# Attention heads' outputs made transposed, with the probabilities scaled before they are turned

## What is computed

```python
# block 0: 8 MoBA heads (with 256 rows: causal softmax attention) and 8 stick-breaking heads
y_a = softmax(mask(q_a @ k_a.T * 64**-0.5)) @ v_a                  # per head, HEAD_DIM 64
A[t,s] = sigmoid(z[t,s]) * prod_{s<j<t} (1 - sigmoid(z[t,j])); y_b = A @ v_b
merged = sigmoid(g_a) * (y_a @ w_branch_moba) + sigmoid(g_b) * (y_b @ w_branch_sb)
x = x + merged @ w_out
# block 1: 8 "fox" heads (softmax with cumulative log-forget bias), 8 "dsa" heads
# (softmax over the 64 best keys of an index score, one shared k and v), same merge
```

## Time and profile before

| | us |
|---|---|
| median of 3 runs (1128.9 to 1129.7) | 1128.99 |
| the profiled execution | 1129.26 |
| its span, first to last instruction | 1127.5 |
| PE busy | 1119.7 |
| DVE busy | 770.7 |
| ACT busy | 621.2 |
| POOL busy | 60.2 |

### The profile page before, as it was taken

One profiled execution on the slowest core, in us unless ns is written; L12 is line 12 of the kernel. 1 busy time (PEld: TensorE's weight loads), 2 busy tenths in 40 slices (PEclk: granted clock), 3 DMA queues, 4 the chain that ended last, 5 costly groups with the idle time before them and its releaser, 6 DMA issues.

```text
span 1127.5 us, 15022 instructions
## 1 busy us (share of the span) xinstructions
PE 1119.7 (99%) x5926; PEld 959.9 (85%) x5926; DVE 770.7 (68%) x1070; ACT 621.2 (55%) x843; POOL 60.2 (5%) x105
## 2 busy tenths in 40 slices
PE   9999999999999999999999999999999999999998
PEld 8888888888888888888888888888788888888887
DVE  6777755754887777775487777457897487777742
ACT  5555532677556456554365555337676864655530
POOL 1000000000000000000000000020253100000000
PEclk9999999999999999999999999999999999999999
DMA  9755565653454565655665555556643445565551
GB/s 316 245 188 188 187 243 192 204 177 119 159 196 149 176 217 187 187 187 187 189 203 186 187 187 188 188 173 248 206 148 115 149 152 184 188 187 187 189 184 38
DMA packets 142581, 208.03 MB, mean 185 GB/s; under 512 B 9296, under 2 KB 100584, under 8 KB 142512
## 3 DMA queue, kind: packets, MB, share of 16 engines
q1 hardware_dynamic: 139408, 198.07, 53.8%
q0 software_dynamic: 3088, 9.00, 2.4%
q10 hardware_dynamic: 16, 0.00, 0.0%
HBM read 205.98 MB, written 2.65 MB: 185 GB/s over the span
## 4 chain that ended last, share of the span: by engine, by line
PE 95%; DVE 2%; ACT 1%; issue 1%; DMA 1%; SPq 0%; ACTq 0%; DVEq 0%
PE banks L1770 26%; PE banks L1631 16%; PE banks L1633 16%; PE banks L1632 16%; PE banks L1768 13%; PE banks L1703 1%; PE banks L1653 1%; PE banks L1918 1%; PE banks L1945 1%; PE banks L1946 1%; DVE w_lo L1107 1%; DMA raw<-in_ffn_w_gate 1%; PE banks L1905 0%; PE banks L1944 0%; PE banks L1872 0%
## 5 line engine op out<-in xcount | busy, mean ns | idle before, releaser
L1107 DVE TENSOR_TENSOR w_lo<-raw,w_hi 128x2048 fp32r<-128x2048 f32 x186 | 423.4, 2279 | 171.9 <-ACT w_hi L731 171.4
L731 ACT ACTIVATE w_hi<-raw 128x2048 fp32r<-128x2048 f32 x186 | 352.7, 1898 | 115.6 <-PE banks L1633 112.1
L1770 PE MATMUL banks<-xT,w_hi 128*128 128x512 f32 x1280 | 313.6, 391 | 0.0
L1770 PEld LDWEIGHTS banks<-xT,w_hi 128*128 128x128 f32 x1280 | 232.6, 189 | 43.3
L1631 PE MATMUL banks<-w_hi,xT 128*128 128x512 f32 (+1 forms) x464 | 183.2, 395 | 1.2 <-DVE w_lo L1107 1.2
L1633 PE MATMUL banks<-w_hi,xT 128*128 128x512 f32 (+1 forms) x464 | 179.3, 387 | 0.0
L1632 PE MATMUL banks<-w_lo,xT 128*128 128x512 f32 (+1 forms) x464 | 179.1, 386 | 0.0
L1768 PEld LDWEIGHTS banks<-xT,w_lo 128*128 128x128 f32 x1280 | 169.9, 191 | 9.6
L1768 PE MATMUL banks<-xT,w_lo 128*128 128x256 f32 x1280 | 173.6, 283 | 0.0
L1631 PE MATMUL banks<-w_hi,hT_hi 128*128 128x512 f32 x352 | 137.3, 390 | 0.0
L1633 PE MATMUL banks<-w_hi,hT_lo 128*128 128x512 f32 x352 | 137.0, 389 | 0.0
(11 more groups left out here) (302 smaller groups left out, 926.1 us busy)
## 6 DMA issues: line engine op xcount, KB each, us to landing
raw<-in_ffn_w_gate SPq DMA_DIRECT2D x88, 512.0 KB, 4.0
raw<-in_ffn_w_up SPq DMA_DIRECT2D x88, 512.0 KB, 5.0
raw<-in_ffn_w_down SPq DMA_DIRECT2D x88, 512.0 KB, 4.3
raw<-in_w_in SPq DMA_DIRECT2D x76, 512.0 KB, 4.6
raw<-in_w_out SPq DMA_DIRECT2D x16, 512.0 KB, 4.4
raw<-in_w_branch_moba SPq DMA_DIRECT2D x4, 512.0 KB, 4.7
raw<-in_w_branch_sb SPq DMA_DIRECT2D x4, 512.0 KB, 6.0
raw<-in_w_branch_a SPq DMA_DIRECT2D x4, 512.0 KB, 4.4
```

Source lines behind the costliest of these rows:

```text
L731: act.activation(w_hi[u % SLOTS][:, 0:n], raw[u % RAWS][:, 0:n], ACT.Copy).then_inc(hi_done, 1)
L1107: dve.tensor_tensor(w_lo[r][:, 0:n], raw[r][:, 0:n], w_hi[u % SLOTS][:, 0:n], ALU.subtract).then_inc(lo_done, 1)
L1770: m = pe.matmul(bank[b + s], mh, xT[:, k].rearrange("p a s -> p (a s)"), start=k == 0, stop=k == KC - 1)
```

## The change

The values become the stationary operand of a head's product: two heads' values side by side, 128 columns (for dsa, whose value is shared, the value twice), so that the output of a head appears transposed, on the 64 partitions of its half, as 256 columns. The first product takes 256 columns of the turned probabilities, the second 128. The reciprocal can't be applied to rows of a transposed output any more, so the probabilities are multiplied by it before they are transposed: on DVE right behind the reciprocal for moba and dsa, on ACT for fox. Transposing, product and copy-out stand one slot later. The copy-out is one copy of 64 x 256 without a factor, for both kinds of heads. PE's transpositions of the branches and their bank reads go; ACT and DVE round and split the collected outputs from SBUF, in two halves a branch, in the slots `Y_AT`.

```diff
-TY_AT = (38, 43)
+Y_AT = [(37, 38, 40, 42), (37, 38, 40, 43)]
@@ items_of
-    out += [(TY_AT[0], "TY", (0, 0)), (TY_AT[0] + 1, "TY", (0, 1)), (TY_AT[1], "TY", (1, 0)), (TY_AT[1], "TY", (1, 1))]
@@
-SM_AT = dict(soft=1, turn=2, out=3, norm=4)
+SM_AT = dict(soft=1, exp=2, scale=3, turn=3, out=4, norm=5)
@@ ACT
-                            mv(dv[:, tt, :], src[:, 72:136])
+                            mv(dv[:, tt, 0:HD], src[:, 72:136])
+                            mv(dv[:, tt, HD:2 * HD], src[:, 72:136])
+                def scale_probs(it):
+                    k, e = 2 * (it.m % 8), prob[it.m % 2]
+                    act.wait_ge(inverted, it.softs + 1)
+                    act.activation(e[:, 0:P], e[:, 0:P], ACT.Copy, scale=rowinv[:, k:k + 1])
+                    act.activation(e[:, P:SC], e[:, P:SC], ACT.Copy, scale=rowinv[:, k + 1:k + 2]).then_inc(scaled_a, 1)
                 def finish_head(it):
...
                     act.wait_ge(head_out, it.m + 1)
-                    if it.kind == "SM":
-                        k = 2 * (it.m % 8)
-                        act.wait_ge(inverted, it.softs + 1)
-                        act.activation(y[br][:, 0, c], O[:, 0:HD], ACT.Copy, scale=rowinv[:, k:k + 1])
-                        act.activation(y[br][:, 1, c], O[:, HD:P], ACT.Copy, scale=rowinv[:, k + 1:k + 2])\
-                            .then_inc(head_read, 1)
...
+                    act.activation(y_cols[br][r, h // 2, :], head_bank(it)[r, 0:SEQ], ACT.Copy).then_inc(head_read, 1)
-                def y_turned(it):
...
+                def y_round(br, n):
+                    heads = [it for it in HEADS if it.b == b and branch_of(it) == br]
+                    act.wait_ge(head_read, heads[4 * n + 3].m + 1)
                     if br == 1:
                         act.wait_ge(unit_used, BASE[ph] + 2 * PROJ)
...
+                    k = slice(2 * n, 2 * n + 2)
+                    act.activation(yT_hi[br][:, k, :], y_cols[br][:, k, :], ACT.Copy).then_inc(y_hi, 1)
@@ ACT, loop over slots: copy_turned, finish_head, then
+                    if slot in Y_AT[b]:
+                        y_round(*divmod(Y_AT[b].index(slot), 2))
...
                     for it in ITEMS[b]:
-                        if it.kind == "SM" and slot - it.slot == SM_AT["turn"]:
+                        if it.kind == "SM" and slot - it.slot == SM_AT["exp"]:
                             exps(it)
+                    for it in ITEMS[b]:
+                        if it.kind == "SM" and it.what[0] == "fox" and slot - it.slot == SM_AT["scale"]:
+                            scale_probs(it)
@@ DVE
                     dve.reciprocal(rowinv[:, k:k + 2], rowsum[:, k:k + 2]).then_inc(inverted, 1)
+                    if it.what[0] != "fox":
+                        e = prob[it.m % 2]
+                        dve.wait_ge(inverted, it.softs + 1)
+                        dve.tensor_scalar(e[:, 0:P], e[:, 0:P], rowinv[:, k:k + 1], None, ALU.mult)
+                        dve.tensor_scalar(e[:, P:SC], e[:, P:SC], rowinv[:, k + 1:k + 2], None, ALU.mult)\
+                            .then_inc(scaled_d, 1)
+                def y_rest(br, n):
+                    dve.wait_ge(y_hi, 4 * b + 2 * br + n + 1)
...
-                        if it.kind == "TY" and d == 1:
-                            y_turned(it)
+                    if slot in Y_AT[b][0:3]:
+                        y_rest(*divmod(Y_AT[b].index(slot), 2))
...
                         merge(0, (0, 1))
+                        y_rest(1, 1)
@@ PE
                 def turn_probs(it):
-                    pe.wait_ge(exped, it.softs + 1)
+                    if it.what[0] == "fox":
+                        pe.wait_ge(scaled_a, it.what[1] + 1)
+                    else:
+                        pe.wait_ge(scaled_d, 8 * b + it.what[1] + 1)
@@ PE, head
-                    O = head_bank(it)[:, SC:NB]
-                    pe.matmul(O[:, 0:HD], w[:, 0:P], v[:, 0, :], start=True, stop=True)
-                    pe.matmul(O[:, HD:P], w[:, P:SEQ], v[:, 0, :], start=True, stop=False)
-                    pe.matmul(O[:, HD:P], w[:, SEQ:SC], v[:, 1, :], start=False, stop=True).then_inc(head_out, 1)
+                    O = head_bank(it)
+                    pe.matmul(O[:, 0:SEQ], v[:, 0, :], w[:, 0:SEQ], start=True, stop=False)
+                    pe.matmul(O[:, P:SEQ], v[:, 1, :], w[:, SEQ:SC], start=False, stop=True).then_inc(head_out, 1)
-                def y_turn(it):
...
@@ PE, branch
-                    ty = [t for t in ITEMS[b] if t.kind == "TY" and t.what == (br, tt)][0]
-                    pe.wait_ge(read_d, ty.read)
...
+                    for k4 in range(4):
+                        if q == 0 and k4 % 2 == 0:
+                            pe.wait_ge(y_lo, 4 * b + 2 * br + k4 // 2 + 1)
```

More of the change, by code:

```diff
@@ L222, in build @@
         y = [mb("y_a", [P, TT, HW]), mb("y_b", [P, TT, HW])]
+        y_cols = [t.rearrange("p a c -> p (a c)").rearrange("p (k t) -> p k t", k=4) for t in y]
         stat = [mb(f"stat{i}", [P, 4, SEQ], F32R) for i in range(2)]
@@ L246, in build @@
         ik_twice, ik_rest = twice[1][:, 0, :], rest[1][:, 0:2, :]
-        dv = mb("dv", [P, TT, HD])
+        dv = mb("dv", [P, TT, 2 * HD])
         index, work = gate[:, 1, DM:DM + SC], gate[:, 0, DM:DM + SC]
@@ L383, in build @@
         y_hi = sem("y_hi")
+        y_lo = sem("y_lo")
+        scaled_a = sem("scaled_a")
+        scaled_d = sem("scaled_d")
         cum_out = sem("cum_out")
@@ L487, in norm_part, with branch_of @@
             return slice(0, 18) if k == 0 else slice(18, 34)
+        def branch_of(it):
+            return 0 if it.what[0] in ("moba", "fox") else 1
         def head_bank(it):
@@ L1005, in relu @@
                                    scale=HD ** -0.5).then_inc(read_a, 1)
-                def y_turned(it):
-                    br, tt = it.what
-                    act.wait_ge(scored, it.i + 1)
+                def y_round(br, n):
+                    heads = [it for it in HEADS if it.b == b and branch_of(it) == br]
+                    act.wait_ge(head_read, heads[4 * n + 3].m + 1)
                     if br == 1:
                         act.wait_ge(unit_used, BASE[ph] + 2 * PROJ)
-                    act.activation(yT_hi[br][:, :, tt * P:(tt + 1) * P],
-                                   bank[4 + it.i % 2][:].rearrange("p (k t) -> p k t", k=4),
-                                   ACT.Copy).then_inc(y_hi, 1)
+                    else:
+                        act.wait_ge(scored, HEADS[15 if b == 0 else 23].i + 1)
+                    k = slice(2 * n, 2 * n + 2)
+                    act.activation(yT_hi[br][:, k, :], y_cols[br][:, k, :], ACT.Copy).then_inc(y_hi, 1)
                 for slot in range(LAST_SLOT):
                     j, q = divmod(slot, 4)
-                    for it in ITEMS[b]:
-                        if it.kind == "TY" and slot - it.slot == 1:
-                            y_turned(it)
                     for it in ITEMS[b]:
@@ L1506, in turn_rest @@
                     ins.then_inc(read_d, 1)
[L1508 to L1513, removed]
+                def y_rest(br, n):
+                    dve.wait_ge(y_hi, 4 * b + 2 * br + n + 1)
+                    k = slice(2 * n, 2 * n + 2)
+                    dve.tensor_tensor(yT_lo[br][:, k, :], y_cols[br][:, k, :], yT_hi[br][:, k, :],
+                                      ALU.subtract).then_inc(y_lo, 1)
                 def merge(br, qs=range(4)):
@@ L1547, in mixer @@
                             sb_keep(it)
-                        if it.kind == "SM" and d == SM_AT["out"]:
+                        if it.kind == "SM" and d == SM_AT["scale"]:
                             invert(it)
@@ L1890, in values @@
                         return dv[:]
-                    return (v_b if kind == "sb" else v_a)[:, :, h * HD:(h + 1) * HD]
+                    return (v_b if kind == "sb" else v_a)[:, :, h // 2 * P:(h // 2 + 1) * P]
                 def scores(it):
@@ L1987, in branch @@
                         pe.wait_ge(merged, 8 * b + q + 1)
-                    m = four(u, tt, bank[2 * n + tt][:], 0, True, True, hi=yT_hi[br], lo=yT_lo[br])
+                    for k4 in range(4):
+                        if q == 0 and k4 % 2 == 0:
+                            pe.wait_ge(y_lo, 4 * b + 2 * br + k4 // 2 + 1)
+                        mh, ml = rows(u, NB, k4)
+                        m = three(bank[2 * n + tt][:], lambda z: z[:, k4, tt * P:(tt + 1) * P], yT_hi[br], yT_lo[br],
+                                  mh, ml, k4 == 0, k4 == 3)
                     m.then_inc(unit_used if tt else tile_done, 1)
@@ L1993, in mixer @@
                     j, q = divmod(slot, 4)
[L1994 to L1997, removed]
                     if j < PROJ:
@@ L2015, in mixer @@
                             scores(it)
-                        if it.kind == "TY" and d == 0 and slot != TY_AT[1]:
-                            y_turn(it)
                 def turn_merged(q):
```

16 lines of the change are left out of this document (2 added, 14 removed).

## The result

| | before | changed |
|---|---|---|
| median of 7 runs, us | 1128.99 (1128.72 to 1129.7) | 1132.75 (1131.73 to 1134.06) |
| profiled execution, us | 1129.26 | 1134.01 |
| its span, us | 1127.5 | 1132.2 |
| PE busy, us | 1119.7 | 1119.0 |
| matmul instructions | 5926 | 5830 |

The changed kernel is slower by 0.36%: ratio 1.0036, 95% interval 1.0026 to 1.0045. The forecast was 1132.4 us. Two things matter. PE is busy a little less, although the kernel takes longer (that answers the earlier trace rows): the loss is above all idle time. And the executions lie 2.3 us apart, where those of before lie within 1.0 us.

What follows compares the result with a forecast made beforehand. PE's dense stream was taken to bound the kernel, so its work and new waits add to the time. Transpositions -3.5, products +0.3 and new waits +6.6 make +3.4 us: 1132.4 us, range 1128.4 to 1135.6 us.

Steps and rivals of the forecast that it cites:

- PE's own work: Whole kernel: removed transpositions save 3.5 us, the new head products add 0.3 us, so PE's work falls by 3.2 us.
- Place 1: Block 0, first head: PE waits 1.35 us for VectorE's reciprocal and scaling.
- Place 2: Block 1, first fox head: PE waits 2.15 us for VectorE's late reciprocal and ScalarE's scaling.
- Place 3: Block 1, second fox head: PE waits 0.9 us because work queued on ScalarE was held behind the first head's reciprocal.
- Other fox heads: Block 1, later fox heads: 0.5 us and more in hand but for one, for which 0.1 us is added.
- Place 4: Block 1, last fox head: its reciprocal stands behind the two selections on VectorE, and PE waits 2.1 us.
- Moved at nothing: Copy-outs, branches' rounding and rest, Pool's normalisation: moved without cost; the fourth rounding, 0.4 us ahead, costs up to 1 us if late.
- Scaling's price on VectorE: Scaling on VectorE: 0.28 us for 128 and 0.35 us for 256 columns, 0.6 us together.
- The cover holds: Rival: the queues turn out looser, no new wait appears, only PE's saved work is left, 1125.8 us; chance 0.12.
- Only the opening waits: Rival: waits only at block 0's first head and the first fox head, later ones covered, 1129.3 us; chance 0.18.
- The hold-up spreads: Rival: ScalarE, once late, holds later heads too; three or four waits of 0.8 us make 1135.4 us; chance 0.14.
- Transpositions at their duration: Rival: the 32 removed transpositions save 0.27 us each, 8.7 us in place of 3.5, time 1127.2 us; chance 0.04.

Runs made afterwards that it cites:

- Experiment 1: Changed kernel with the scaling of the probabilities left out and PE's transpositions waiting for the exponentials alone: 1125.44 us, ratio to before 0.9969.
- experiment 2: Experiment 1 with 32 transpositions put back, 16 behind the last head of each block, results unused: 1129.30 us.
- experiments 3: Changed kernel with all moba and fox reciprocals a slot earlier in VectorE's queue, moba's with its scaling: 1126.25 us, ratio 0.9976.
- experiment 5: Changed kernel with the reciprocal of the first fox head alone a slot earlier: 1130.15 us.
- experiment 7: Changed kernel with the reciprocals of the last two fox heads alone at the start of the slot before: 1130.60 us.
- experiment 9: Changed kernel with two more copies by a factor of 1 on ScalarE for each fox head: 1136.83 us, one execution.
- changed again (8): The changed kernel run again as it is, beside other runs on the same chip: 1133.63 us.
- experiment 4: Changed kernel with the reciprocal and scaling of the moba heads alone a slot earlier: 1132.35 us, against 1133.63 us on the same chip.
- experiment 6: Changed kernel with ScalarE's scaling of the first fox head moved behind its slot's copy-out and weight split: 1134.45 us, one execution.

## Why the prediction was right

**What bounds.** PE's stream does; each wait shows up whole in the time. Right.

**PE's own work, -3.2 us.** The ledger leaves -3.2 us for it. Experiment 1 agrees: its profiled execution gains 3.8 us, of which 0.5 us are old waits gone and 0.5 us an earlier start of the first products, against 0.5 us of waits that are new or longer, which leaves 3.3 us. The transpositions' step was right (0.11 us by the rows and by experiment 2); the head came to 0.64 to 0.66 us for my 0.65. Two slips in the working touched nothing: there are six groups of transpositions, not four, and 32 in all as counted; and the lower bound of 0.60 us a head makes -1.3 us, not -0.9.

**Place 1**: forecast 1.35, measured 1.42 us. **Place 2**: 2.15 and 2.38 us. My scaling of 0.7 us on ScalarE took 0.8 (829.29 to 830.09); PE's arrival against the reciprocal came out as forecast. **Place 3**: 0.9 and 0.82 us. The number is right, the reason only in part: I put the whole wait down to ScalarE being held, and by experiments 3 and 5 0.5 us of it are there without that, from ScalarE's own work in the slot. **Other fox heads**: 0.1, measured 0.04 us, at the sixth. **Place 4**: 2.1 and 1.99 us. The sum was 6.6 us, and 6.6 us were measured; counted as the forecast counted them, from the start at which PE would have gone on to the start at which it did, the four come to 1.36, 2.31, 0.77 and 1.94 us, 6.4 in all. What made this possible is that the ends on VectorE's side at places 1 and 2 hang on nothing that the change touches, so they could be read from the trace of before.

**Moved at nothing.** Right: no wait of PE on the branches' rests or on Pool's work appears in the changed kernel, the fourth rounding included.

**Scaling's price on VectorE**: 0.28 and 0.35 us were taken. The rows at place 1 agree (0.29 and 0.35); the means over all sixteen heads are 0.34 and 0.44 us. No wait came of it.

**The sum.** Forecast +3.4 us, measured +3.8 us by the medians. Part of the nearness is luck: two errors point in opposite directions. Without the half clock the changed kernel takes 1131.7 to 1131.8 us (the lowest executions of both series), 2.7 to 3.1 us above before, so my sum was 0.3 to 0.7 us too high; it had no term for old waits that the change makes vanish, and these are 0.5 us. The half clock, which I did not have at all, adds 0.7 to 2.6 us in ten executions of twelve. The step that failed is the silent one: a wait was priced at its own length, and PE's clock behind it at full speed.

**The rivals.** "The cover holds" fell with the time and the waits. "Only the opening waits" fell too: the fourth place is 2 us by itself (experiment 7). It was right in one point, found in another way: whatever delays PE behind place 2, here the half clock, does hide the third wait. "The hold-up spreads" did not happen; in experiment 9, with one more scaling a head, two later heads wait (0.27 and 1.42 us), so it was not far away. "Transpositions at their duration" fell with experiment 2.

## What to carry to other kernels

When an operation moves from the end of a chain into its middle, look not at its length but at where it stands in its engine's program: the reciprocal took 0.17 us, and its late place most of 6.6 us. Walk the consumer's arrival against the producer's end for the first and the last item of each series, where another kind of work stands in the queue, and move the operation to the point where its input is ready (here one slot earlier, for a few lines: 1126.25 us in place of 1131.7 at full clock, 1132.75 by the medians).

If the engine that was held has itself little to spare, part of the wait stays. Price a product or a transposition in a dense stream by the distance between ends. An idle second of the bottleneck engine may cost more than itself.

## What the runs showed of the hardware

A wait of PE can take clock with it. In a kernel that is busy throughout, with a granted clock of 1.00, eight of twelve idle times of 1.78 us or more were followed by 3.41 us at half clock (1.2 GHz):

| profiled execution | idle time of PE, and when half clock began after PE went on, us |
|---|---|
| changed | 2.15: none; 1.78: 1.4 |
| changed again (8) | 2.14: none; 1.78: 1.0 |
| experiment 4 | 2.17: 0.0; 1.78: 1.3 |
| experiment 5 | 1.78: none |
| experiment 6 | 2.38: 0.2; 1.79: 1.5 |
| experiment 7 | 2.18: 0.6 |
| experiment 9 | 2.95: 0.6; 1.42: none; 3.20: none |

The length of the wait alone does not decide: 3.20 us brought none and 1.78 us did, four times of five. What decides stays open. After the waits of 1.2 us in block 0 no profile shows one. Filling the waits at the first and last fox head with useless products kept the clock at 0.999 to 1.000 in six executions, which lay within 0.7 us of each other.

A transposition of 128 x 128 in fp32 lasts 0.27 us and costs 0.11 us in a dense stream (32 of them moved what follows by 3.55 us). Plain fp32 products of 64 columns cost as much per instruction as those of 128 (0.11 us), so that doubling the columns and dropping one product of three left the head's cost where it was.
